# Reordering five waits in a two-block transformer kernel: stick-breaking exponentials, heads of the last attention, a bank for its output rows, and a shorter norm statistic

## The reference

```
h = h + 0.5 * rmsnorm(swiglu(rmsnorm(h, g0)), g1)
h = h + rmsnorm(mixer(rmsnorm(h, g2)), g3)        # layer 0: retention, layer 1: stick-breaking attention
h = h + 0.5 * rmsnorm(swiglu(rmsnorm(h, g4)), g5)
h = h + rmsnorm(sigmoid(rmsnorm(h, g6) @ w_gate) * (p @ w_proj), g7)
```

## Time and profile before

| | |
|---|---|
| median of 3 runs | 1376.66 us |
| the profiled execution, its own time | 1376.57 us |
| span from its first to its last instruction | 1374.8 us |
| mean granted TensorE clock | 1.000 |
| TensorE matmul (PE) busy | 1365.8 us, 99% |
| TensorE weight load (PEld) busy | 1156.2 us, 84% |
| VectorE (DVE) busy | 942.9 us, 69% |
| ScalarE (ACT) busy | 724.0 us, 53% |
| GpSimd (POOL) busy | 129.8 us, 9% |
| DMA | 251.04 MB, mean 183 GB/s |
| chain of work that ended last | PE 91%, DVE 5%, ACT 1%, POOL 1%, issue 1% |

### The profile page before, as it was taken

One profiled execution on the slowest core, in us unless ns is written; L12 is line 12 of the kernel. 1 busy time (PEld: TensorE's weight loads), 2 busy tenths in 40 slices (PEclk: granted clock), 3 DMA queues, 4 the chain that ended last, 5 costly groups with the idle time before them and its releaser, 6 DMA issues.

```text
span 1374.8 us, 19708 instructions
## 1 busy us (share of the span) xinstructions
PE 1365.8 (99%) x6920; PEld 1156.2 (84%) x6920; DVE 942.9 (69%) x1136; ACT 724.0 (53%) x991; POOL 129.8 (9%) x177
## 2 busy tenths in 40 slices
PE   8999999999999999999999999999999999999999
PEld 7888888888888888888888888888888888888787
DVE  6777768677667776577777454677775676577675
ACT  6444455445454444475445366654444565545674
POOL 0111010000011110010110011111110110002100
PEclk9999999999999999999999999999999999999999
DMA  8656646555646666447666454455567456555431
GB/s 259 206 183 199 203 149 208 173 189 191 213 134 195 192 216 224 146 147 233 191 199 230 157 186 151 145 162 183 185 219 239 147 171 203 184 165 184 145 127 67
DMA packets 186960, 251.04 MB, mean 183 GB/s; under 512 B 15589, under 2 KB 115853, under 8 KB 186893
## 3 DMA queue, kind: packets, MB, share of 16 engines
q1 hardware_dynamic: 186604, 250.04, 56.2%
q10 hardware_dynamic: 288, 0.13, 0.0%
HBM read 249.06 MB, written 1.05 MB: 182 GB/s over the span
## 4 chain that ended last, share of the span: by engine, by line
PE 91%; DVE 5%; ACT 1%; POOL 1%; issue 1%; DMA 0%; POOLq 0%; SPq 0%; DVEq 0%; ACTq 0%
PE sums L531 17%; PE sums L529 17%; PE sums L530 17%; PE sums L678 11%; PE turn L678 11%; PE turn L684 6%; PE sums L684 6%; DVE w_lo L1575 2%; PE turn L607 1%; PE turn L529 1%; PE turn L531 1%; PE turn L530 1%; POOL stat L1035 1%; DVE stat L2040 0%; DVE work L2037 0%
## 5 line engine op out<-in xcount | busy, mean ns | idle before, releaser
L1575 DVE TENSOR_TENSOR w_lo<-raw,w_hi 128x1024 fp32r<-128x1024 f32 x460 | 553.4, 1240 | 144.0 <-ACT w_hi L1122 143.2
L1122 ACT ACTIVATE w_hi<-raw 128x1024 fp32r<-128x1024 f32 x460 | 470.3, 1054 | 239.6 <-DMA raw<-in_ffn_w_up_dram 96.6
L529 PE MATMUL sums<-w_hi,x_both 128*128 128x512 f32 x608 | 241.2, 397 | 0.2 <-issue 0.2
L531 PE MATMUL sums<-w_hi,x_both 128*128 128x512 f32 x608 | 237.2, 390 | 0.0
L530 PE MATMUL sums<-w_lo,x_both 128*128 128x512 f32 x608 | 236.8, 389 | 0.0
L529 PE MATMUL sums<-w_hi,y_hi 128*128 128x512 f32 x510 | 200.4, 393 | 0.0
L531 PE MATMUL sums<-w_hi,y_lo 128*128 128x512 f32 x510 | 198.7, 390 | 0.0
L530 PE MATMUL sums<-w_lo,y_hi 128*128 128x512 f32 x510 | 198.5, 389 | 0.0
L678 PE MATMUL sums<-x_both,w_hi 128*128 128x512 f32 x640 | 153.0, 391 | 0.0
L678 PE MATMUL turn<-x_both,w_hi 128*128 128x512 f32 x640 | 152.7, 391 | 0.0
L678 PEld LDWEIGHTS turn<-x_both,w_hi 128*128 128x128 f32 x640 | 117.6, 188 | 22.8
(11 more groups left out here) (220 smaller groups left out, 1285.5 us busy)
## 6 DMA issues: line engine op xcount, KB each, us to landing
raw<-in_ffn_w_gate_dram SPq DMA_DIRECT2D x176, 256.0 KB, 3.6
raw<-in_ffn_w_up_dram SPq DMA_DIRECT2D x176, 256.0 KB, 4.4
raw<-in_ffn_w_down_dram SPq DMA_DIRECT2D x176, 256.0 KB, 3.6
raw<-in_ret_w_in_dram SPq DMA_DIRECT2D x96, 256.0 KB, 4.2
raw<-in_conv_w_in_dram SPq DMA_DIRECT2D x64, 256.0 KB, 3.8
raw<-in_attn_w_in_dram SPq DMA_DIRECT2D x64, 256.0 KB, 3.8
raw<-in_sb_w_in_dram SPq DMA_DIRECT2D x48, 256.0 KB, 3.5
raw<-in_ret_w_out_dram SPq DMA_DIRECT2D x32, 256.0 KB, 4.3
```

The lines of the kernel that those rows point to most:

```text
L529: pe.matmul(bank[:, :], a, wh, start=(first and c == 0), stop=False, skip_group_check=True)
L531: mm = pe.matmul(bank[:, :], b, wh, start=False, stop=(last and c == SC - 1), skip_group_check=True)
L1122: act.activation(w_hi[:, n % RING].rearrange("p c n -> p (c n)"), raw[:, n % RAW].rearrange("p c n -> p (c n)"), ACT.Copy).then_inc(hi_mad ...
L1575: dve.tensor_tensor(w_lo[:, n % RING].rearrange("p c n -> p (c n)"), raw[:, n % RAW].rearrange("p c n -> p (c n)"), w_hi[:, n % RING].rear ...
```

## The change

It has five parts, all in the order or the form of small steps. (1) ScalarE's `out_phase` gets a parameter `early`. In `sb_out` it is 0, so that ScalarE makes the four exponentials and the four `sb_y_hi` before slot base+8, not after it. VectorE's `out_phase` stays as it is. (2) VectorE does stage 0 of the last attention before slots s0+20 and s0+21. (3) In stage 7, ScalarE makes the exponentials of head 15 before `mb_y_hi(0, 1)`, not after it. (4) Rows piece (0,1) is turned into a bank of `sums`, the one that output group 1 will write. So the wait of head 15's transposes for that piece goes, and the wait of `moba_out` for its `y_lo` moves from slot 2 to slot 1. (5) ScalarE's squares are scaled, so that their sums are already divided by 1024 and the weight, and GpSimd makes both additions in one instruction: two steps in place of three, at all 16 statistics of the norms after a phase.

```diff
--- before.py
+++ after.py
@@ -363,6 +363,8 @@
             return rows.rearrange("p (t n) -> p t n", t=2)
 
         def mb_y_bank(half, i):
+            if (half, i) == (0, 1):
+                return sums[(PHASES["moba_out"].group0 + 1) % BANKS]
             return turn[0] if (half, i) == (1, 1) else turn[3]
 
         def mb_p_bank(hd):
@@ -959,8 +961,8 @@
                     pe.wait_ge(mb["pt_flat"], hd - 1)
                 if hd in (2, 3):
                     pe.wait_ge(mb["flat"], 5 + hd)
-                if hd in (13, 15):
-                    pe.wait_ge(y_lo_made, y_base("moba") + (1 if hd == 13 else 2))
+                if hd == 13:
+                    pe.wait_ge(y_lo_made, y_base("moba") + 1)
                 at = MW_HEAD + (hd % 2) * 768
                 for c in range(3):
                     mm = pe.transpose(mb_p_bank(hd)[:, c * P:(c + 1) * P], work[:, at + c * P:at + (c + 1) * P], ident[:, :])
@@ -998,8 +1000,10 @@
 
                 pe.wait_ge(mb["gated"], 2 * half + 2)
                 bank = mb_y_bank(half, i)
-                if (half, i) != (1, 1):
-                    pe.wait_ge(mb["pt_flat"], 12 + 2 * (2 * half + i))
+                if (half, i) == (0, 1):
+                    wait_bank(PHASES["moba_out"], 1)
+                elif i == 0:
+                    pe.wait_ge(mb["pt_flat"], 12 + 4 * half)
                 at = (MW_Q, MW_K)[half]
                 for c in range(2):
                     for t in range(NT):
@@ -1014,7 +1018,7 @@
             hooks.update({8 + k: lambda k=k: mb_stage(k) for k in range(8)})
             in_proj("moba_in", 9, hooks, {10: {2: lambda: mb_turn(1, 1)}, 15: {(3, 0): lambda: mb_turn_y(0, 0)}})
             out_proj("moba_out", None, y_hi, y_lo,
-                     {0: lambda: pe.wait_ge(y_lo_made, yb4 + 1), 2: lambda: pe.wait_ge(y_lo_made, yb4 + 2),
+                     {0: lambda: pe.wait_ge(y_lo_made, yb4 + 1), 1: lambda: pe.wait_ge(y_lo_made, yb4 + 2),
                       4: lambda: pe.wait_ge(y_lo_made, yb4 + 3), 6: lambda: pe.wait_ge(y_lo_made, yb4 + 4)},
                      {0: lambda: (mb_turn_y(0, 1), mb_stage(8)), 1: lambda: mb_stage(9),
                       (3, 0): lambda: mb_turn_y(1, 0), 3: lambda: mb_turn_y(1, 1)})
@@ -1055,12 +1059,12 @@
                     pool.wait_ge(gated_sq, 4 * int(name[-1]) + 2 * t + 2)
                 else:
                     pool.wait_ge(act_read, ph.act0 + 2 * t + 2)
-                pool.tensor_tensor(tmp_post[:, 2 * t:2 * t + 1], f_sq[:, 2 * t:2 * t + 1], f_sq[:, 2 * t + 1:2 * t + 2],
-                                   ALU.add).then_inc(pool_step, 1)
+                pool.tensor_scalar(tmp_post[:, t:t + 1], f_sq[:, 2 * t:2 * t + 1], f_sq[:, 2 * t + 1:2 * t + 2],
+                                   eps_post[:, t:t + 1] if name.startswith("down") else EPS / weight ** 2,
+                                   ALU.add, ALU.add).then_inc(pool_step, 1)
                 step[0] += 1
                 pool.wait_ge(pool_step, step[0])
-                rsqrt(r_post[:, t:t + 1], tmp_post[:, 2 * t:2 * t + 1], tmp_post[:, 2 * t + 1:2 * t + 2],
-                      1.0 / D / weight ** 2, eps_post[:, t:t + 1] if name.startswith("down") else EPS / weight ** 2, r_post_made)
+                pool.tensor_tensor(r_post[:, t:t + 1], tmp_post[:, t:t + 1], neg_half[:, 0:1], ALU.pow).then_inc(r_post_made, 1)
 
             zero = pool.to_reg(0.0)
 
@@ -1159,13 +1163,13 @@
                     act.wait_ge(sums_done, ph.group0 + 2 * t + n + 1)
                     squared(act_read, ph.act0 + 2 * t + n + 1)
                     act.activation(junk[:, 0:COLS], sums[(ph.group0 + 2 * t + n) % BANKS][:, :], ACT.Square,
-                                   accum_out=f_sq[:, 2 * t + n:2 * t + n + 1]).then_inc(act_read, 1)
-
-            def out_phase(name, b, late, read):
+                                   scale=D ** -0.5 / post[name][2], accum_out=f_sq[:, 2 * t + n:2 * t + n + 1]).then_inc(act_read, 1)
+
+            def out_phase(name, b, late, read, early=1):
 
                 ph = PHASES[name]
                 base, free = ph.slot0, ph.slot0 + ph.slots - ph.window + RING
-                split_to(min(base + RING + 1, free))
+                split_to(min(base + RING + early, free))
                 for fn in late:
                     fn()
                 split_to(free)
@@ -1333,7 +1337,7 @@
                         act.wait_ge(gated, 4 * layer + g + 1)
                         squared(gated_sq, 4 * layer + g + 1)
                         act.activation(junk[:, 0:COLS], work[:, EW_S + g * 512:EW_S + (g + 1) * 512], ACT.Square,
-                                       accum_out=f_sq[:, g:g + 1]).then_inc(gated_sq, 1)
+                                       scale=D ** -0.5, accum_out=f_sq[:, g:g + 1]).then_inc(gated_sq, 1)
 
                 out_phase(f"ple_gate{layer}", b + 1, [], read)
 
@@ -1435,7 +1439,7 @@
                 for hd in range(4, 8):
                     sb_y_hi(hd)
 
-            out_phase("sb_out", 6, [sb_late], lambda t: squares("sb_out", t))
+            out_phase("sb_out", 6, [sb_late], lambda t: squares("sb_out", t), early=0)
 
             ffn(3, 6)
             ple(1, 7)
@@ -1504,8 +1508,6 @@
                 if k in (0, 5):
                     act.preload_act_table_set("natural_log_exp_and_others")
                 for hd in range(2 * k, 2 * k + 2) if k < MH // 2 else ():
-                    if hd == MH - 1:
-                        mb_y_hi(0, 1)
                     sm = soft[:, 6 * (hd % 8):6 * (hd % 8) + 6]
                     at = MW_HEAD + (hd % 2) * 768
                     act.wait_ge(mb["max"], 2 * hd + 2)
@@ -1515,6 +1517,8 @@
                         cols = slice(at, at + P) if t == 0 else slice(at + P, at + 384)
                         act.activation(work[:, cols], work[:, cols], ACT.Exp, scale=MDH ** -0.5, bias=sm[:, t:t + 1],
                                        accum_out=sm[:, 2 + t:3 + t]).then_inc(mb["exp"], 1)
+                    if hd == MH - 1:
+                        mb_y_hi(0, 1)
 
             def mb_silu(half):
 
@@ -2098,9 +2102,10 @@
             mb_norm(0, 1)
             split_to(s0 + 20)
             mb_norm(1, 1)
-            split_to(s0 + 22)
             for k in range(8):
                 mb_stage(k)
+                if k == 0:
+                    split_to(s0 + 22)
                 if k == 6:
                     mb_y_lo(0, 0)
                 if k == 5:
```

## The result

17 runs of the changed kernel have a median of 1379.3 us (1377.48 to 1380.51). 17 of the kernel before have 1376.79 us (1376.6 to 1377.24). The 17 runs are not one group. Four have a mean granted TensorE clock of 1.000 and took 1377.48 to 1377.73 us. The other 13 have a clock of 0.999 or 0.998 and took 1379.02 to 1380.51 us. The profiled execution is of the second kind (1379.32 us, clock 0.999).

A forecast was written before the change was run, and what follows sets the result against it. TensorE, busy 1365.8 of 1374.8 us, was taken as the bound. The terms +3.7 - 0.37 - 0.28 - 1.05 - 1.35 - 0.25 = +0.4 us on the median 1376.66 gave 1377.0 us, range 1375.9 to 1379.4.

The forecast's parts named there:

- the likeliest case: Whole kernel: the forecast itself, 1377.0 us with its own range 1376.3 to 1379.1; chance 0.74.
- the rival of the falling clock: In sb_out, the new wait brings back TensorE's half rate, costing 3.0 us more: 1380.0 us; chance 0.13.
- matmuls follow each other by over 0.4 us after the wait: TensorE in sb_out after the new wait: spacing over 0.4 us, listed as a sign the forecast is wrong.
- L874: TensorE's products with v in sb_out: no idle before this line, listed as a sign of right.
- the two GpSimd rows: Norm statistic on GpSimd: two rows before each h, listed as a sign of right.
- the last L966: TensorE's transposes at the last heads: the idle before the last one is gone, listed as a sign of right.
- L607: TensorE's turning of h after the gated embeddings: late by 0.1 to 0.3 us, a sign of right.
- The new wait: TensorE at slot 4 of sb_out: waits 3.7 us for y_lo in a closed loop, bounds 3.4 to 4.1.
- Stick-breaking exponentials: sb_out: exponentials start earlier, so TensorE's products with v are no longer late; gain 0.37 us.
- First heads: Last attention: stage 0 before two slots ends TensorE's lateness in stage 1; gain 1.35 us, bounds 1.0 to 1.35.
- Norm statistic: One GpSimd step fewer: gain 0.28 us at the end of sb_out, 1.05 us after the gated embeddings.
- Last heads: Last heads and bank: wait for head 15 goes, a smaller y_lo wait comes; gain 0.25 us, bounds 0 to 0.38.

The follow-up runs named there:

- 1373.87: Changed kernel with ScalarE's slot base+8 after the four exponentials but before the four copies: 1373.87 us, ratio 0.998.
- 1373.92: Changed kernel with VectorE's order changed like ScalarE's, its four y_lo before its slot base+8: 1373.92 us, ratio 0.998.
- the two timed kernels: Changed kernel with the early exponentials undone (1374.5 us), and changed kernel with ScalarE's slot base+8 between exponentials and copies (1373.87 us).
- the longer wait: Changed kernel with VectorE's slot base+9 also before its four y_lo: 1381.12 us, ratio 1.003.
- the shorter: Changed kernel with ScalarE's slot base+8 after the copies of heads 4 and 5, before those of 6 and 7: 1376.4 us, ratio 1.0002.
- the seven variants without that wait: Early exponentials undone 1374.5, base+8 between exponentials and copies 1373.87, VectorE reordered 1373.92, norm alone 1376.06, stage 0 alone 1375.23, last heads and bank alone 1376.5, later bank 1373.62.

## Why the prediction was right, and where it was not

The forecast was 1377.0 us, no change by 0.2%. The measured 1379.3 us is inside the range of 1375.9 to 1379.4 and inside 0.2%, but not by the likeliest case: in 13 of 17 runs the rival of the falling clock came on top of it. That the median is still inside, by 0.1 us, is luck: this rival was put at 1380.0, outside the range, and its price was too high. The sign "matmuls follow each other by over 0.4 us after the wait", listed under wrong, came (0.43, eight times). The signs of the wait itself, of L874, of the two GpSimd rows, of stage 1 and of the last L966 came as listed under right. L607 was late by 0.42 and 0.31 after the embeddings, both above the 0.1 to 0.3 named. The ends of the sum are also added wrongly. By the stated bounds they are -0.2 (3.4 - 0.37 - 0.3 - 1.2 - 1.35 - 0.38) and +1.9 (4.1 - 0.37 - 0.2 - 0.6 - 1.0 - 0), not -0.3 and +2.4. That gives 1376.5 to 1378.6, and with the same margin of 0.3 on top the range would have missed 1379.3.

- **The new wait** was the term that decided, and it was right: 3.7 forecast, 3.58 measured, released by `y_lo` as said. The links of the loop stand in the timelines: from where slot 4 would have begun (887.94) to the split of base+8 1.64 (1.65 forecast), the split 1.14 (1.18), two `y_lo` and the restart 0.80 (0.87). Each way of cutting or lengthening it gave the time worked out beforehand (1373.87, 1373.92, a wait of 2.27 for 2.3, one of 4.73 for 4.7).
- **Stick-breaking exponentials, gain** 0.37: the idle time before the products is gone and their first pair is 0.10 quicker too, 0.47 together in the trace, 0.6 between the two timed kernels (there the idle time was 0.42, not 0.21).
- **First heads**: 1.35 forecast, 1.35 in the trace, 1.36 alone. Slots s0+20 and s0+21 were covered as costed.
- **Norm statistic** was mis-sized: 0.28 + 1.05 forecast, 0.10 + 0.60 in the account, 0.53 alone. The step that failed is "the changed first step is of the kind of the 0.19 row". It is drawn at 0.29, and the power starts 0.38 after it, not 0.28. From the first step to the update of h it takes 1.05 us (899.72 to 900.77) where it took 1.22: a saving of 0.17, where the prediction counted 0.28 five times (the last time held to about 0.2). Five times 0.17 is 0.85, so why 0.70 and 0.53 came is open. The Trainium skill (Perfetto Trace Analysis, "GPSIMD Engine Instruction") would have spacing rather than drawn length used. The trace agrees as far as it goes, but the spacing of another form was the wrong one to take.
- **Last heads**: 0.25 forecast, 0.07 in the account, 0.09 alone. What is late next was named rightly (`y_lo` of the piece), but TensorE started slot 1 at 1353.18, 0.30 after that `y_lo` ended (1352.88), where the prediction added almost nothing. Using the bank of group 3, which also lets the wait for `y_lo` come later, removes the whole of it. Why TensorE resumes 0.05 after its releaser in sb_out and 0.30 after it here stays open. The profile puts 0.31 of idle before the weight load of this matmul down to "issue".
- **Without the clock** the sum is +0.8 us (1377.48 to 1377.73 in the four runs at 1.000, against 1376.79) where +0.4 was forecast. The account of the two traces makes it 3.58 - 0.47 - 0.10 - 0.60 - 1.35 - 0.07 = +1.0. That is 0.6 above the forecast: the norm (0.6) and the last heads (0.2), less the wait and the exponentials (0.2). The 0.2 between the account and the timed runs is not explained.
- **The falling clock** had its mechanism right and both numbers off. Its chance of 0.13 was far too low (13 of 17 runs, 5 of 6 with that part alone, 7 of 7 with the longer wait, 4 of 11 with the shorter, and none of the other 76 runs of the seven variants without that wait; of the other 77 runs of the kernel before beside the experiments, one had 0.999 and took 1378.81 us). Its price of 3.0 was too high: 1.6 in the profiled execution, 1.4 to 2.9 over the runs (1379.02 to 1380.51 less 1377.58, the middle of the four). The 6.1 us at half rate of the start were taken for it, and the slow stretch went from 892.35 to 895.74 here.

The Trainium skill (TensorE: Matmul & The Clock Gate, "Part 1: The HAM clock gate") gives the rule that an idle stretch brings the half clock. The windows agree: granted 0.50 after the wait of 3.58 us, and within the wait of 4.73 us. With a wait of 2.27 us, 4 of 11 runs have a mean clock of 0.999 and took 1.5 to 2.1 us more than the median of the other seven (1376.24), though no trace shows where their clock fell.
